# Row-wise output norms and a norm folded into the convolution's eviction in a two-layer decoder step

## The reference, cut to what matters

```python
x = x + rmsnorm(mixer(rmsnorm(x)))
x = x + rmsnorm(convffn(rmsnorm(x)))

def conformer_conv(x, buf, w_in, b_in, dw_w, dw_b, ln_w, ln_b, w_out, b_out):
    h = x @ w_in + b_in
    h = h[..., :C] * sigmoid(h[..., C:])
    h, new_buf = causal_dwconv(h, buf, dw_w, dw_b)     # width 31
    h = silu(layernorm(h, ln_w, ln_b))
    return h @ w_out + b_out, new_buf
```

## Time and profile before

| what | us |
| --- | --- |
| median of 3 runs | 1931.82 (1930.93 to 1933.19) |
| the profiled execution | 1930.9 |
| its span, first to last instruction | 1929.1 |
| PE busy in the span | 1808.1 (94%) |
| DVE busy | 1137.4 (59%) |
| ACT busy | 510.4 (26%) |
| POOL busy | 530.0 (27%) |
| mean granted clock of PE, share of 2.4 GHz | 0.973 |

### The profile page before, as it was taken

One profiled execution on the slowest core, in us unless ns is written; L12 is line 12 of the kernel. 1 busy time (PEld: TensorE's weight loads), 2 busy tenths in 40 slices (PEclk: granted clock), 3 DMA queues, 4 the chain that ended last, 5 costly groups with the idle time before them and its releaser, 6 DMA issues.

```text
span 1929.1 us, 43248 instructions
## 1 busy us (share of the span) xinstructions
PE 1808.1 (94%) x18475; PEld 1613.9 (84%) x18475; DVE 1137.4 (59%) x1913; ACT 510.4 (26%) x875; POOL 530.0 (27%) x512
## 2 busy tenths in 40 slices
PE   6999998999999979999999996999897999999998
PEld 5767778888887669999999994776576998999998
DVE  6148324655655137866838456999306884856836
ACT  2136222222223233322222222011424322222213
POOL 0000000121213134545445442000014544444443
PEclk8999989999998989999999998999998999999999
DMA  5211200000001421223232321221021223223222
GB/s 160 77 33 55 69 0 3 15 15 8 11 14 34 96 71 56 73 71 97 71 104 71 89 79 43 66 59 50 24 66 44 77 68 99 80 82 88 60 83 79
DMA packets 228796, 117.69 MB, mean 61 GB/s; under 512 B 26321, under 2 KB 226473, under 8 KB 228489
## 3 DMA queue, kind: packets, MB, share of 16 engines
q1 hardware_dynamic: 227243, 114.85, 21.2%
q10 hardware_dynamic: 1390, 0.44, 0.1%
HBM read 109.31 MB, written 6.67 MB: 60 GB/s over the span
## 4 chain that ended last, share of the span: by engine, by line
PE 76%; DVE 14%; issue 6%; ACT 2%; DVEq 1%; DMA 1%; SPq 0%; ACTq 0%; POOL 0%
PE ps L882 32%; PE ps L535 26%; PE ps L671 12%; PE ps L612 2%; PE ps L1008 2%; DVE tmp L1466 1%; DVE arena L1494 1%; DVE arena L1862 1%; DVE arena L1678 1%; DVE arena L1866 1%; DVE arena L1680 1%; DVE arena L1845 1%; DVE x L1498 1%; DVE arena L1871 1%; PE ps L546 1%
## 5 line engine op out<-in xcount | busy, mean ns | idle before, releaser
L882 PE MATMUL ps<-hsplit,wsplit 128*128 128x288 f32 x4224 | 575.8, 298 | 33.2 <-DVE hsplit L1501 25.9
L882 PEld LDWEIGHTS ps<-hsplit,wsplit 128*128 128x128 f32 x4224 | 571.1, 191 | 36.7 <-issue 22.5
L535 PE MATMUL ps<-arena 128*128 128x288 f32 (+1 forms) x1728 | 429.4, 411 | 14.5 <-ACT arena L1440 6.5
L535 PEld LDWEIGHTS ps<-arena 128*128 128x128 f32 (+1 forms) x1728 | 328.8, 191 | 114.5 <-issue 15.0
L2016 POOL TENSOR_TENSOR wsplit<-arena,wsplit 128x1024 fp32r<-128x1024 f32 (+2 forms) x152 | 324.0, 2136 | 331.6 <-ACT wsplit L1285 331.3
L882 PE MATMUL ps<-hidsplit,wsplit 128*128 128x288 f32 x2112 | 288.1, 298 | 7.9 <-DVE arena L1847 5.3
L882 PEld LDWEIGHTS ps<-hidsplit,wsplit 128*128 128x128 f32 x2112 | 285.1, 191 | 9.0 <-DVE arena L1847 5.7
L671 PE MATMUL ps<-arena 64*64 64x64 f32 (+2 forms) x7008 | 267.1, 229 | 22.6 <-DVE arena L1678 13.1
L671 PEld LDWEIGHTS ps<-arena 64*64 64x64 f32 x7008 | 238.8, 137 | 42.8 <-DVE arena L1678 18.2
L1285 ACT ACTIVATE wsplit<-arena 128x1024 fp32r<-128x1024 f32 (+2 forms) x152 | 142.0, 943 | 301.9 <-PE ps L882 230.8
L1865 DVE SCALAR_TENSOR_TENSOR arena<-arena,par 128x512 f32<-128x512 f32 x176 | 160.6, 912 | 22.6 <-DVE arena L1862 5.5
(11 more groups left out here) (217 smaller groups left out, 1655.0 us busy)
## 6 DMA issues: line engine op xcount, KB each, us to landing
arena<-ffn_w_in SPq DMA_DIRECT2D x88, 512.0 KB, 3.9
arena<-ffn_w_out SPq DMA_DIRECT2D x48, 384.0 KB, 3.5
arena<-conv_w_in SPq DMA_DIRECT2D x16, 512.0 KB, 4.0
arena<-rwkv_wk SPq DMA_DIRECT2D x8, 512.0 KB, 7.8
arena<-rwkv_wr SPq DMA_DIRECT2D x8, 512.0 KB, 4.0
arena<-rwkv_wv SPq DMA_DIRECT2D x8, 512.0 KB, 4.0
arena<-rwkv_wo SPq DMA_DIRECT2D x8, 512.0 KB, 4.4
arena<-ffn_w_out SPq DMA_DIRECT2D x16, 256.0 KB, 2.8
```

What stands on the lines that cost most here:

```text
L535: ins = pe.matmul(ps[0:m, o:o + HALF], lhs, rhs[:, HALF * z:HALF * z + HALF], start=st, stop=sp)
L882: ins = pe.matmul(ps[:, s + 512 * z:s + 512 * z + HALF], lhs(u, i), rhs[:, v, j, HALF * z:HALF * z + HALF], start=i == 0 and n == 0, stop= ...
```

## The change

n1, n3 and n5 get `row_norm`: PE multiplies the two terms of the sum with a single column, for eight groups of 72 tokens, so that the mean squares lie as 72 x 8 values with tokens on partitions. ACT and DVE take root and reciprocal of these, DVE multiplies an identity with them (72 x 576), and eight matmuls with the constant matrix spread the scale to all partitions, from where ACT copies it. n4 is folded into the convolution: ACT writes h = gain times x without the scale, PE runs the first three GLU tiles block by block as h comes, with n4's sum in front of the last block, and DVE, not ACT, evicts the GLU tiles and multiplies by n4's scale. The sigmoid follows from SBUF, and biases enter at DVE's products. The history's transposes come before n3, their eviction is DVE's, their copies are ACT's. The output product runs in split parts as the FFN's, with the splits of four weights behind the last sigmoid on ACT and behind the diagonals on POOL. The arena is laid out anew, and some waits go with that. The core of the diff:

```diff
-SQ_NORMS = ["n1", "n2", "n3", "n5", "n6", "n7"]
+ROWS, ROW_NORMS = 72, ["n1", "n3", "n5"]
+SQ_NORMS = ["n1", "n2", "n3", "n4", "n5", "n6", "n7"]
-GLU_EVERY = 15
+GLU_EVERY = 10
...
@@ sync @@
-                eng.wait_ge(sm["tile_full"], TB[("wo", "co")[l]] + KT - 2)
+                if l == 0:
+                    eng.wait_ge(sm["tile_full"], TB["wo"] + KT - 2)
+                else:
+                    eng.wait_ge(CV["w_lo"], KT - 2)
-            eng.wait_ge(sm["tile_full"], TB["d0"] + 1)
+            eng.wait_ge(sm["tile_full"], TB["fo0"] + 2)
...
-            weights("co", a["conv_w_out"][0], range(RING))
+            for j in range(KT):
+                if j < RING:
+                    eng.wait_ge(sm["tile_full"], WTILE[WB["co"] + j - RING] + 1)
+                else:
+                    eng.wait_ge(CV["w_lo"], j - RING + 1)
+                wtile(WB["co"] + j, a["conv_w_out"][0], j)
...
@@ tensor @@
+            def row_norm(name):
+                n, t = ROW_NORMS.index(name) + 1, TB[name]
+                begin(t)
+                for g in range(NG):
+                    for i, (lhs, rhs, pre) in enumerate(sum_terms(name)):
+                        for w, v in pre:
+                            pe.wait_ge(w, v)
+                        ins = pe.matmul(row_sum(name)[:, g:g + 1], rhs[:, ROWS * g:ROWS * g + ROWS], lhs[:, 0:1], start=i == 0, stop=i == 1)
+                ins.then_inc(sm["row_sums"], 1)
+                pe.wait_ge(sm["row_diag"], n)
+                for g in range(NG):
+                    o = tset(t) + 512 * (g // 4) + ROWS * (g % 4)
+                    ins = pe.matmul(ps[:, o:o + ROWS], con[0:ROWS, C_MEAN:C_MEAN + P], row_diag[:, g, :], start=True, stop=True)
+                ins.then_inc(sm["tile_full"], 1)
-            product(TB["n1"], sum_terms("n1"))
+            row_norm("n1")
...
-                    product(TB["n3"], sum_terms("n3"))
+                    pe.wait_ge(sm["gst_in"], 48)
+                    for t in range(4):
+                        transposes(TB["gst"] + t, [grows[:, g, :] for g in range(4 * t, min(4 * t + 4, NGG))])
+                    row_norm("n3")
...
-            norm_sums("n4")
-            gemm("glu", h, (sm["h_ready"], 0))
+            t0 = TB["glu"]
+            begin(t0 + LOOK - 1)
+            for kt in range(KT):
+                if kt == KT - 1:
+                    product(TB["n4"], sum_terms("n4"))
+                pe.wait_ge(sm["h_ready"], kt + 1)
+                for j in range(LOOK):
...
+                    ins = halves(t0 + j, ring[:, w % RING, kt, :], h[:, kt, :], kt == 0, kt == KT - 1)
...
+            gemm("glu", h, None, first=LOOK)
+            def out_product():
+                t0 = TB["co"]
+                begin(t0 + LOOK - 1)
+                pe.wait_ge(CV["w_lo"], LOOK)
+                for kt in range(KT):
+                    pe.wait_ge(CV["z_lo"], kt + 1)
+                    for j in range(LOOK):
+                        ins = parts(t0 + j, weight(j), hsplit, kt, KT)
...
+                for j in range(LOOK, KT):
+                    begin(t0 + j)
+                    pe.wait_ge(CV["w_lo"], j + 1)
+                    split_product(t0 + j, weight(j % 4), hsplit, KT)
-            gemm("co", cvo, (sm["z_ready"], 0))
-            product(TB["n5"], sum_terms("n5"))
+            out_product()
+            row_norm("n5")
@@ scalar @@
+            def row_root(name):
+                act.wait_ge(sm["row_sums"], ROW_NORMS.index(name) + 1)
+                f(row_r, row_sum(name), ACT.Sqrt, bias=con[0:ROWS, C_EPS:C_EPS + 1]).then_inc(sm["row_sqrt"], 1)
+                take(TB[name])
+                freed(f(two(tmp[:, 2, :]), wide(TB[name]), ACT.Copy))
+            def conv_w_hi(j):
+                w = WB["co"] + j
+                act.wait_ge(w_in[w % RING], 16 * (w // RING + 1))
+                if j >= 4:
+                    act.wait_ge(sm["tile_full"], TB["co"] + j - 3)
+                f(wsplit[:, j % 4, 0], ring[:, w % RING], ACT.Copy).then_inc(CV["w_hi"], 1)
...
+                    if l == 1 and n < KT - 4:
+                        conv_w_hi(n + 4)
-                root(norm_name)
+                row_root(norm_name)
                 w_hi(l, 2)
...
-            norm("n4", x, (sm["x_ready"], KT))
+            for kt in range(KT):
+                act.wait_ge(sm["x_ready"], KT + kt + 1)
+                f(h[:, kt, :], x[:, kt, :], ACT.Copy, scale=gain(4, kt)).then_inc(sm["h_ready"], 1)
+                square("n4", kt, x[:, kt, :])
+            root("n4")
             for n in range(KT):
...
-                freed(f(two(gsig[:, 1, :]), wide(ta), ACT.Identity, bias=pcol("conv_b_in", n)))
-                freed(f(two(gsig[:, 0, :]), wide(tb), ACT.Sigmoid, bias=pcol("conv_b_in", KT + n)))
+                f(gd[:, n, :, 0:NSTATE], gs[:, n], ACT.Copy).then_inc(sm["hist_copied"], 1)
+                act.wait_ge(sm["tile_read"], TB["glu"] + 2 * n + 2)
+                f(gsig[:, 0, :], gsig[:, 0, :], ACT.Sigmoid, bias=pcol("conv_b_in", KT + n)).then_inc(sm["sig_ready"], 1)
+            for j in range(4):
+                conv_w_hi(j)
...
                 f(cvo[:, kt, :], cvo[:, kt, :], ACT.Silu, scale=pcol("conv_ln_w", kt), bias=pcol("conv_ln_b", kt)).then_inc(sm["z_ready"], 1)
+                act.wait_ge(sm["z_ready"], kt + 1)
+                f(hsplit[:, 0, kt, :], cvo[:, kt, :], ACT.Copy).then_inc(CV["z_hi"], 1)
@@ vector @@
-                norm_scale(name)
+                dve.wait_ge(sm["row_sqrt"], row)
+                seq(v.reciprocal(row_r, row_r))
+                after()
+                v.scalar_tensor_tensor(row_diag, ident[0:ROWS, 0:ROWS].unsqueeze(1).to_broadcast([ROWS, NG, ROWS]), float(D),
+                                       row_r.unsqueeze(2).to_broadcast([ROWS, NG, ROWS]), ALU.mult, ALU.mult).then_inc(sm["row_diag"], 1)
+                dve.wait_ge(sm["tile_read"], TB[name] + 1)
...
-            prenorm("n4", 4)
+            norm_scale("n4", dst=rs4)
             def glu(kt):
...
-                seq(v.tensor_tensor(gb[:, kt, NSTATE:NSTATE + SEQ], gsig[:, 1, 0:SEQ], gsig[:, 0, 0:SEQ], ALU.mult))
+                dve.wait_ge(sm["tile_full"], ta + 1)
+                v.tensor_tensor(two(gsig[:, 1, :]), wide(ta), two(rs4), ALU.mult).then_inc(sm["tile_read"], 1)
+                dve.wait_ge(sm["tile_full"], tb + 1)
+                v.tensor_tensor(two(gsig[:, 0, :]), wide(tb), two(rs4), ALU.mult).then_inc(sm["tile_read"], 1)
+            def gate_rows(kt):
...
+                dve.wait_ge(sm["sig_ready"], kt + 1)
+                dve.wait_ge(sm["hist_copied"], kt + 1)
+                seq(v.scalar_tensor_tensor(gb[:, kt, NSTATE:NSTATE + SEQ], gsig[:, 1, 0:SEQ], b, gsig[:, 0, 0:SEQ], ALU.add, ALU.mult))
...
-                    late = [decode_sum, decode_bias]
+                    late = [gate_rows, decode_rows, decode_sum, decode_bias]
...
+            for kt in range(KT):
+                dve.wait_ge(CV["z_hi"], kt + 1)
+                v.tensor_tensor(hsplit[:, 1, kt, :], cvo[:, kt, :], hsplit[:, 0, kt, :].bitcast(F32), ALU.subtract).then_inc(CV["z_lo"], 1)
             postnorm("n5", 5, (6, 1))
@@ gpsimd @@
+            def conv_w_lo(j):
+                w = WB["co"] + j
+                pool.wait_ge(CV["w_hi"], j + 1)
+                p.tensor_tensor(wsplit[:, j % 4, 1], ring[:, w % RING], wsplit[:, j % 4, 0].bitcast(F32), ALU.subtract).then_inc(CV["w_lo"], 1)
...
                     add_square(("n1", "n5")[l], kt)
+                    if l == 1 and kt < 5:
+                        conv_w_lo(kt + 3)
...
-            pool.wait_ge(sm["tile_full"], TB["gst"] + 4)
+            for kt in range(1, KT - 1):
+                add_square("n4", kt)
+            pool.wait_ge(sm["x_ready"], 2 * KT)
             for m, kt in enumerate(DW_PE):
...
+            for j in range(4):
+                conv_w_lo(j)
             ffn(1)
```

More of the change, by code:

```diff
@@ L260, in build @@
         cvo = region(A_CO)
-        gsig = region(A_SIG, 2)
+        gsig = hg
+        rs4 = arena[:, A_RS:A_RS + T]
         gd = gb[:, :, NSTATE + SEQ:GB].rearrange("p k (b t) -> p k b t", b=DB)
@@ L329, in build @@
                                            "h_hi", "h_lo", "hid32_ready", "hid_hi", "hid_lo")} for l in range(2)]
+        CV = {n: sem(f"{n}c") for n in ("w_hi", "w_lo", "h_hi", "h_lo", "z_hi", "z_lo")}
         block = ctx.enter_context(nc.Block())
@@ L504, in _ @@
             store(out["s_glu"][0, :, 0:NSTATE - DS, :], a["state_conv_glu"][0, :, DS:NSTATE, :])
-            weights("co", a["conv_w_out"][0], range(KT), first=RING)
             ffn(1)
@@ L1389, in ffn @@
                 if l == 0:
-                    root("n3")
+                    row_root("n3")
             ffn(0)
-            for t in range(4):
-                m = min(512, NGS - 512 * t)
-                take(TB["gst"] + t)
-                freed(f(gst[:, 512 * t:512 * t + m], bank2(TB["gst"] + t, m), ACT.Copy))
-            norm("n4", x, (sm["x_ready"], KT))
-            for n in range(KT):
```

(32 more changed lines are left out.)

58 lines of the change are left out of this document (37 added, 21 removed).

## The result

The changed kernel takes 1937.98 us (median of 19 runs, 1934.48 to 1940.78) beside 1931.82 for the kernel before (19 runs): a ratio of 1.0031, 95% interval 1.0024 to 1.0038. It is slower, by a third of a per cent. The profiled execution took 1939.46 us, in the upper half of its runs, with a span of 1937.7 against 1929.1.

What follows compares the result with a forecast made beforehand. The prediction took TensorE's work and the steps it waits for as the bound. Its terms, 3.8 + 7.6 - 5.4 + 3.8 = +9.8 on 1930.9, gave 1940.7, with 0.9 to the median 1941 us; range 1924 to 1949.

Steps and rivals of the forecast that it cites:

- row sums: In each row norm: 16 single-column matmuls, 32 trace records at 0.113 us each, taking 3.6 us on TensorE.
- spread: In each row norm: 8 matmuls, 16 records with 128-column weights at 0.113 us, taking 1.8 us.
- hold by the weight split, n1 and n5: GpSimd's half of the third FFN weight's split would run beside VectorE's scaling and hold it, 2.1 us lost each.
- n3 to the first GLU matmul: After norm n3 the first GLU matmul would start at 1172.1 instead of 1190.17, 18.1 us earlier.
- VectorE's end of the conv stage, from n3: VectorE's added evictions, sigmoid waits and held operations would move its last copy from 1352.05 to 1368.7.
- TensorE's transposes, from n3: TensorE, through its taps at 1347.0, would wait for VectorE; transposes start at 1368.7 instead of 1363.07, +5.6 us.
- start at the low clock: After 20 us without work before the transposes, TensorE would restart at the low clock, charged 2 us.
- low parts of z; output product: Low parts behind eight VectorE multiplications delay the first output matmul by 4.5 us; the split product saves 9.9; together -5.4.
- rival (a): Row norms: a 72-column load costs less than a 128-column one, saving 1 us per norm; 1938 us, chance 0.15.
- Rival (b): Weight splits don't hold VectorE at six places (n1, n5, four in the taps), 12.6 us; 1929 us, chance 0.18.
- (c): Conv stage: VectorE is not the end, TensorE goes on at 1347; 1918 us, chance 0.07.
- (d): Conv stage: ACT's copies queue behind late weight loads, putting TensorE's end at 1379; 1951 us, chance 0.08.

## Why the prediction was right

Forecast: 1941 us, slower; measured 1937.98. The steps, in us:

| step | predicted | measured |
|---|---|---|
| row sums | 3.6 | 2.4 in n1, 2.2 in n3, 2.1 in n5 |
| spread | 1.8 | 3.7 in n1 and n3, 3.0 in n5 |
| hold by the weight split, n1 and n5 | 2.1 each | 2.15 each |
| n1, n5 in all | +3.8 each | +4.5, +3.5 |
| n3 to the first GLU matmul | -18.1 | -18.05 |
| VectorE's end of the conv stage, from n3 | +16.65 | +14.0 |
| TensorE's transposes, from n3 | +5.6 | +3.1 |
| start at the low clock | +2 | +2.25 |
| low parts of z; output product | +4.5; -9.9 | +4.45; -11.2 |
| conv stage and product in all | +2.2 | -1.1 |
| first FFN; second FFN and end | 0; 0 | +2.5; -1.4 |

**The nearness of the total is in part luck.** The three stretches were forecast at +3.8, +2.2 and +3.8 and measured at +4.5, -1.1 and +3.5; what had been put at nothing (both FFNs and the time ahead of n1) came to +1.6. The misses of -3.3 and +1.6 run against each other. The traces are 8.6 us apart and the medians 6.2, and the sum of the prediction itself, 1940.7 and 0.9, is 1941.6, not 1941.

**The norm.** Its direction was right for partly the wrong reason: two terms were off, against each other. The sums were priced by the row with mostly 128-column loads, 0.113 us a record; the 30 loads with 72 columns took 2.29 in n1, 0.076 each. The Trainium skill ("TensorE: Matmul & The Clock Gate", section "LDWEIGHTS (loading the stationary operand)") has a load take as long as its columns; an estimate by it is 60 ns for 72 columns, which is nearer to the measured 76, the figure that decides here, than the price I kept. By itself that would have made rival (a). But the low clock, which I named as a bound and didn't take "since PE comes straight from full work", is what the spread met: in n1 it cost 1.9 and the sums saved 1.2, in n5 1.2 against 1.5.

**The held operations.** Both prices of 2.1 came from one row, and two experiments give them back: 2.15 at each place in n1 and n5, 6.4 in the taps. There the forecast had 8.4, four splits at 2.1; only three lay beside operations that are held, and the reduction at 1328.88 ran unheld at 2.21 beside the fourth. The Trainium skill ("SBUF — State Buffer", section "SBUF: two separate sides") lets a GpSimd operation that reads SBUF and a VectorE operation that reads two tensors from it run only one at a time; the decode product and the taps read two, the reduction one, and the trace agrees (2.86, 6.01 and 2.88 against an unheld 2.21). Rival (b) is out.

**The convolution stage.** VectorE became the end, as forecast, so rivals (c) and (d) are out. Counted from the end of one VectorE operation to the end of the next, idle time included, the evictions cost 10.7 (16 by 0.67), the sigmoid waits 7.2 (8 by 0.90), the products with bias 1.6 and the holds 6.5, against 10.9, 6.4, 0.9 and 8.4; the start came 7.2 earlier instead of 7.45. That is 18.8, and 14.0 were measured. The taps gave 3.1 instead of 2.5, and 1.7 came from a term that the sum doesn't have: a tap now stands between any two decode steps of a block too, where the reduction used to follow its product directly. The history copies that moved to ACT gave nothing: they lay in the 11.60 us that VectorE waited for its first product. With the output product 1.3 us better than its term, the stage ended 3.3 us ahead of the forecast.

**What was costed at nothing.** The first FFN, from n2's reciprocal to n3's last square, is 2.5 us longer in this execution, and 0.7 to 2.4 longer in the nine other profiles with row norms, 0.7 in the second one of the unchanged kernel; in the three with the old norms it is 417.6, as before. Some 1.6 of the 2.5 go with where the granted clock falls: in the three profiles at 419.9 to 420.1 us it is at 0.50 for a while from 65 us and again from 116 us behind n2's reciprocal, in the kernel before and in the ten others from 102 to 104 us (in one of them, 418.75, from 65 us as well). The second FFN has the same two pictures: 436.4 to 436.6 us in four profiles, that of the kernel before among them, which have the later fall at 115 us, and 435.0 to 435.1 in the ten others, at 102 to 104. So the 1.4 us by which it is shorter here isn't shown to come from the change. What makes the clock fall there, and which wait the other 0.7 to 0.9 us of the first FFN are, stays open.

## What to carry to other kernels

A small operation that takes the place of a wide one must be priced with the steps that carry its result back: a reciprocal of 0.20 us instead of 3.75 bought a diagonal product, a spread, a copy and two more handovers between engines, and lost. When work moves to another engine, ask first what slack that engine had: VectorE had 11 us here, the work moved to it and the waits that came with it took 18, and TensorE spent most of its 18 us head start idle. And before moving a step on ACT or GpSimd, look at which VectorE operation its GpSimd half will lie beside: three such places were worth 10.7 us.

## What the runs showed of the hardware

- The granted clock fell to its lower level in the middle of single-column matmuls that ran without a gap (1.00, 0.65, 0.50 from 705.5 to 707.1). With 64 columns, at the same duration, it stayed at 1.00 in n1, in one profile. That the number of columns is the cause isn't shown: with wide sums it fell in n3 and n5, and with single columns it held now and then there.
- Work in a pause kept the clock for what followed (7.93 us against 10.24), and the fall came at the next pause instead (0.66 from 1366 to 1376).
- An operation of VectorE that reads two tensors from SBUF took 2.1 to 2.2 us longer beside a GpSimd split (0.75 to 2.90, 3.77 to 6.01), one that reads a single tensor didn't (2.21). GpSimd is held in its turn: the split that began under the operation of 6.01 us took 5.97 instead of 2.4.
- A matmul record with a 72-column load takes the same 0.07 to 0.08 us with 1 moving column and with 64 (30 in 2.11 us at full clock in n5, and in 2.16).
